# Attention: ScalarE takes the statistics of the older item ahead of its copy of the newer transposed map

## The reference, cut to what matters

```python
logits = jnp.einsum('bqhmd,bkhmd->bmhqk', q[:, q0:L], k[:, :L]) * scale + bias
logits = jnp.where(dist >= 0, logits, -jnp.inf)
probs = jax.nn.softmax(logits, axis=-1)
attn = (probs[:, 0] - lam * probs[:, 1])
outs.append(jnp.einsum('bhqk,bkhe->bqhe', attn, v[:, :L]))
...
o = rmsnorm(o, subln_g) * (1.0 - lambda_init)
```

## Time and profile before

| What | us |
|---|---|
| median of three runs (lowest, highest) | 1913.54 (1906.49, 1918.45) |
| profiled execution, its own time | 1910.36 |
| span of the profiled execution, first to last instruction | 1908.5 |
| first `normed` to last `normed` in `attend` (L736) | 367.1 to 495.0 |
| busy in the span: PE, DVE, ACT, POOL | 1715.7, 1458.1, 1185.1, 522.5 |

### The profile page before, as it was taken

One profiled execution on the slowest core, in us unless ns is written; L12 is line 12 of the kernel. 1 busy time (PEld: TensorE's weight loads), 2 busy tenths in 40 slices (PEclk: granted clock), 3 DMA queues, 4 the chain that ended last, 5 costly groups with the idle time before them and its releaser, 6 DMA issues. The chain is left out here.

```text
span 1908.5 us, 34291 instructions
## 1 busy us (share of the span) xinstructions
PE 1715.7 (90%) x10549; PEld 1382.9 (72%) x10549; DVE 1458.1 (76%) x1966; ACT 1185.1 (62%) x1802; POOL 522.5 (27%) x363
## 2 busy tenths in 40 slices
PE   2998999777599977998699999999999999999994
PEld 2787887545388856776478887887888788888783
DVE  6587651587478756667499989988898889998897
ACT  4411121477466533333388888887888788888886
POOL 0011100000022200336333433343443343335431
PEclk9999999999699978999799999999999999999997
DMA  9266710300200063528889978799979999799966
GB/s 357 87 199 202 209 54 23 136 16 17 96 3 12 15 227 102 112 80 138 234 290 301 291 229 290 238 331 327 290 252 300 318 309 292 263 313 312 302 199 200
DMA packets 132669, 380.04 MB, mean 199 GB/s; under 512 B 27509, under 2 KB 40142, under 8 KB 130524
## 3 DMA queue, kind: packets, MB, share of 16 engines
q1 hardware_dynamic: 97276, 288.36, 43.7%
q0 software_dynamic: 35312, 90.60, 18.8%
HBM read 334.38 MB, written 82.13 MB: 218 GB/s over the span
## 5 line engine op out<-in xcount | busy, mean ns | idle before, releaser
L2491 DVE TENSOR_TENSOR w_low<-w_experts,w_high 128x2048 fp32r<-128x2048 f32 x194 | 444.1, 2290 | 65.2 <-ACT w_high L2423 60.7
L2423 ACT CAST w_high<-w_experts 128x2048 fp32r x195 | 373.7, 1917 | 6.6 <-SPq L2350 6.6
L2405 POOL DMA_INDIRECT acc<-y_rows,idx x96 | 210.1, 2189 | 532.0 <-DMA acc<-y_rows,idx 289.0
L2500 DVE TENSOR_TENSOR w_low<-w_experts,w_high 128x2048 fp32r<-128x2048 f32 x96 | 219.5, 2286 | 19.8 <-ACT w_high L2432 19.7
L2568 PE MATMUL rbank<-w_high,xT_high 128*128 128x512 f32 x776 | 205.2, 406 | 1.1 <-issue 1.1
L2568 PE MATMUL rbank<-w_low,xT_high 128*128 128x512 f32 x776 | 194.8, 393 | 0.0
L2568 PE MATMUL rbank<-w_high,xT_low 128*128 128x512 f32 x776 | 194.6, 392 | 0.0
L2432 ACT CAST w_high<-w_experts 128x2048 fp32r x96 | 183.7, 1914 | 0.0
L2387 POOL DMA_INDIRECT gathered<-h,idx x97 | 168.1, 1733 | 44.3 <-issue 24.7
L2568 PEld LDWEIGHTS rbank<-w_low,xT_high 128*128 128x128 f32 x776 | 145.7, 188 | 33.9
L2568 PEld LDWEIGHTS rbank<-w_high,xT_low 128*128 128x128 f32 x776 | 145.7, 188 | 32.9
(11 more groups left out here) (440 smaller groups left out, 3397.1 us busy)
## 6 DMA issues: line engine op xcount, KB each, us to landing
w_experts<-in_exp_w SPq DMA_DIRECT2D x384, 512.0 KB, 7.9
qT<-in_w_ada POOLq DMA_DIRECT2D x16, 1024.0 KB, 6.5
w_raw<-in_w_in SPq DMA_DIRECT2D x24, 512.0 KB, 6.5
w_ada<-in_w_ada SPq DMA_DIRECT2D x16, 512.0 KB, 15.1
p_mixed<-mixed SPq DMA_DIRECT2D x8, 512.0 KB, 8.3
w_out<-in_w_out SPq DMA_DIRECT2D x1, 4096.0 KB, 12.4
x_kept<-x SPq DMA_DIRECT2D x8, 512.0 KB, 8.4
acc_tile<-acc SPq DMA_DIRECT2D x8, 512.0 KB, 7.0
```

The source lines that it names most:

```text
L2405: pool.indirect_dma_start(dr["acc"], bass.IndirectOffsetOnAxis(ap=idx[j][:, 0:1], axis=0), y[j % 2][:], None, bounds_check=S - 1, oob_is_e ...
L2423: act.copy(w13_s[par][0][:, a], w13[:, bass.ds(w, 1), a].squeeze(1)).then_inc(w_high, 2)
L2491: dve.tensor_tensor(w13_s[par][1][:, a], w13[:, bass.ds(w, 1), a].squeeze(1), w13_s[par][0][:, a], ALU.subtract).then_inc(w_low, 2)
L2500: dve.tensor_tensor(w2_s[1][:], w2[:, bass.ds(w, 1)].squeeze(1), w2_s[0][:], ALU.subtract).then_inc(d_low, 1)
```

## The change

The change moves one call in ScalarE's list: stats(r-3) now stands at the head of the round, before the first copy of item r-2. Nothing is added or taken away, and no wait is edited.

```diff
             for r in range(N + 3):
+                if r >= 3:
+                    stats(r - 3)
                 if 2 <= r < N + 2:
                     copy_half(r - 2, 0)
-                if r >= 3:
-                    stats(r - 3)
                 if 2 <= r < N + 2 and ITEMS[r - 2][1] >= 4:
                     copy_half(r - 2, 1)
                 if r < N:
                     exponentials(r)
```

## The result

The changed kernel took 1894.23 us (median of five runs, 1890.20 to 1900.79) against 1907.32 us for the kernel before (five runs, two of them added to the three of above, 1906.49 to 1918.45). The ratio is 0.9933, with a 95% interval of 0.9908 to 0.9959: 13 us or 0.7% faster, within the 1% that the prediction gave as its likeliest class. The prediction held that a change under 1% can't be told from none; the interval leaves 1 out, so this one can. 1901 us was forecast with a range of 1893 to 1910, so the time fell inside the range but at its low end. Of the 6.8 us between forecast and result 4.5 belong to the starting point, not to the change: the forecast started from 1911.8 us (1901 + 10.8), between the profiled execution and the median of three, and the median of five is 1907.32.

What follows compares the result with a forecast made beforehand. In `attend`, a loop of combine, transposes, copy, statistics and normed was taken to bound rounds where VectorE idles. Rounds 7.2, drain 2.1 and clock 1.5 sum to 10.8 us saved, giving 1901 us, range 1893 to 1910.

Steps and rivals of the forecast that it cites:

- The rounds: In `attend`, earlier statistics shorten the intervals between `normed` starts: 2.0 us a head, 7.2 us over the stage.
- the longest of three things: Each `normed` interval: VectorE's own work; the loop normed, output, statistics; or exponentials outlasting the output, plus 1.06 us.
- The 0.08 us of overlap: Added to VectorE's own work, since an instruction that does not wait starts about 0.08 us before the previous one's shown end.
- The clock: At items 6 and 22, most of the loss from TensorE's slow clock goes: 1.5 us, between 0 and 2.2.
- The drain: At the stage's last items, earlier `normed` lets output 31 start near 490.6 us, not 492.71: 2.1 us saved.
- What the copy pays: The newer item's copy stands behind 0.94 us of statistics, hidden by the output's wait for `normed`: cost 0, up to 0.94.
- The sign that the prediction named: On ScalarE, the copy of a long item starts directly behind L679, the statistics; no size given.
- What lies behind: In the stages after `attend`, each engine starts anew after the block's end, so the shift passes through undiminished.
- The slower case: On the 16 long items, the delayed copy becomes the late one: up to 0.94 us each, 1925 us; chance 0.06.
- Half the gain taken back: Earlier `normed` makes the output's second copy or VectorE's scores wait last: gain 2 to 7 us, about 1906; chance 0.20.
- no change: Statistics ready no earlier, as the outputs end last: 0 ± 2 us, 1911 us; chance 0.05.
- The rival of more than forecast: Clock stays up from `attend` into the following stage: over 15 us gained, 1895 us; chance 0.07.

Runs made afterwards that it cites:

- e9: Against the changed kernel, the first small operation of the statistics stands ahead of the wait for the output; 1889.82 us, ratio 0.9930 to the kernel before.
- e10: Against the changed kernel, VectorE takes combine ahead of normed; 1892.83 us in one run, 30.53 and 30.54 us a head.
- e8: Against the changed kernel, three extra small copies ahead of a long item's first copy; 31.96 us a head against 30.30, stage 142.1 us.

## Why the prediction was right, point by point

**The rounds.** The step that gave each interval as the longest of three things held to a few hundredths at n = 7, 6 and 4. Measured at full clock: n = 7 3.54 (forecast 3.54), n = 6 3.32 (3.32), n = 4 3.36 (3.37), and 4.58, 4.18 and 4.44 for n = 3, 0 and 2, unchanged. Two were mis-sized, both where VectorE's own work is the bound: n = 1 came at 3.78 (3.87 to 3.95 in the prediction) and n = 5 at 3.10 (3.19 to 3.27). The 0.08 us of overlap had the wrong sign. The idle time in a row counts from the end shown for the instruction ahead, and one that does not wait starts 0.08 us before that end, so the overlap goes off as well: 4.02 - 0.15 - 0.08 = 3.79 and 3.80 - 0.61 - 0.08 = 3.11. With 3, 4, 4, 4 and 3 intervals the savings at full clock are 0.81 + 1.96 + 0.96 + 2.80 + 1.47 = 8.0 us, not 7.2.

**The clock** was forecast at 1.5 us and gave 1.25: the two falls of before gave back 0.71 and 1.48 us, and a new one at item 14, with what it left over for item 16, cost 0.62 + 0.32. How many falls one launch has is luck as far as these profiles tell: the second profile of the change had no such fall, the whole 2.2 us came back, and its first to last `normed` took 114.4 us against 115.1. What I wrote of it, that most of the loss goes even if the clock falls there again, was too hopeful: the interval of item 14 took 3.98 us with the fall and 3.36 without, because the output itself (2.50 us for 1.38) is in the new loop.

**The drain** is the term that was off: 2.1 us forecast, 3.5 measured. The timeline of both engines in the changed kernel, items 30 and 31, answers to the earlier trace rows:

```profile
472.31 1.34 PE L779 MATMUL ps_o<-v,attnT 128*128 128x128 f32 x10
...
474.74 0.35 DVE L736 SCALAR_TENSOR_TENSOR o<-ps_o,soft_stats,subln 128x128 f32<-128x128 f32 x1 [1.95 <-ACT soft_stats L679]
...
475.32 1.13 PE L779 MATMUL ps_o<-v,attnT 128*128 128x128 f32 x8 [1.24 <-ACT attnT L671]
...
477.54 0.35 DVE L736 SCALAR_TENSOR_TENSOR o<-ps_o,soft_stats,subln 128x128 f32<-128x128 f32 x1 [2.45 <-ACT soft_stats L679]
```

The order of events is the one forecast, the last output waiting for its copy and no longer for `normed`. From item 28's `normed` to item 31's it is 8.82 us, before it was 12.34. Output 30 took 1.34 us where I had kept the 2.50 us of the slow clock, and these 1.16 us are most of the 1.4 that the forecast lacked. The granted clock in the drain was 1.00, before 0.74 (windows of the changed kernel and of the kernel before: length, then busy and count of PE, PEld, DVE, ACT and POOL, the clock, DMA share, GB/s):

```profile
466.00:479.00 13.00, 6.54 (x48) 5.53 (x48) 6.22 (x15) 8.41 (x33) 0.00 (x0) 1.00 0.10 27
```

```profile
480.00:496.00 16.00, 8.16 (x44) 6.48 (x42) 5.59 (x13) 7.30 (x30) 0.00 (x0) 0.74 0.06 17
```

This goes with the order and not with one execution: in the kernel before the clock fell on the way to item 30 in both profiles (the drain took 12.34 and 12.81 us), in the changed one in neither (8.82 and 8.83). It stayed up in e9 and e10 too, and fell there in all other variants. So the 3.5 us are the earlier statistics and the clock together, and the prediction's term for the drain had kept the slow clock.

Together: 8.0 + 1.25 + 3.5 = 12.8 us, the measured 127.85 - 115.05 us from first to last `normed`. The forecast was 10.8; the last `normed`, forecast near 484 us, came at 477.54 after a projection stage 4.6 us shorter, so at 482.1 counted from the old start of the stage.

**What the copy pays** was put at 0 under the output's wait. At full clock the rounds came as if the copy cost nothing, and e8 shows that this is cover and not absence of a path. The sign that the prediction named, the copy of a long item directly behind L679, was seen at n = 7 and 4 only; at n = 6 and 5 it waited for its transposes.

**What lies behind** the stage took the shift over whole: 1411.0 and 1412.6 us before, 1412.5 and 1412.0 after, at the same mean clock of 0.96.

**The rivals.** The slower case did not occur; its place was right (the copy of long items), but an extra 0.97 us a copy cost only 1.7 us a head (e8). Half the gain taken back, and no change, are excluded by the stage's 13 to 14 us. The rival of more than forecast, by the clock of the following stage, did not occur. That the clock adds a gain is partly true within the stage: the Trainium skill's rule (TensorE: Matmul & The Clock Gate, What's actually happening), by which activity releases the throttle, put the two falls at 2.2 us; the runs agree with it in tendency only. The shorter the stage, the higher its mean clock (0.86 at 167 us, 0.91 and 0.93 at 147, 0.96 and 0.99 at 134), but a fall itself makes the stage longer, so this does not show which comes first, and one of the two profiles of the change still had a fall.

## What to carry to other kernels

When an engine idles ahead of a step whose input is ready, look at what stands in front of the producer in its own list, and ask which of the two waits it serves ends first; put the one that can start first first, if the other cannot become ready before it. Write the steady state as intervals of one marker instruction, and take each as the longest of the waiting engine's own work, the new loop and the producer's other work; it gave each round of this stage to within 0.1 us of the value taken. When two edits shorten the same wait, do not add their savings: here each gave 1.6 to 2.2 us a head, and both together no more than one.

## What the runs showed of the hardware that was not expected

TensorE's granted clock in a stage of short bursts differs between executions of one kernel: the changed kernel's stage had 0.96 and 0.99. Ahead of the drain, the falls of these two kernels lie at one place of a head, the output of n = 4, where the same ten matrix multiplications take 1.38 or 2.50 us: the kernel before had one at items 6 and 22 in both profiles and none at item 14, though in its first profile TensorE's wait before that output was 1.47 us each time; the change had one at item 14 in one profile and none in the other. What a fall costs depends on the order: 0.71 and 1.48 us before, 0.94 in the changed kernel, 2.9 in e10 (items 22 and 23). Why it falls at one of these places and not at another, these runs do not settle.
